# Expert weights of a mixture-of-experts layer loaded as one 8 KB piece per partition, in place of four pieces of 2 KB or two of 4 KB

## The chip, the core and the metric

The kernel runs on one core of a Trainium2 chip; the other cores are idle. The metric is the device time of one execution in microseconds (us), the median of several runs. The profile is that of one more execution.

## What is computed

One layer of a decoder over 512 tokens of width 1024, all in float32. A first half mixes tokens (an input projection, a retention branch, a recurrent branch, an output projection, a layer norm). The second half is the mixture of experts, and only it is touched here. Cut to that:

```python
expert = g_idx[:, None] * EXPERTS_PER_GROUP + top_i      # two of 32 experts for each token
...
def expert_rows(args):
    xb, e = args
    h = jax.nn.silu(xb @ w_e_gate[e]) * (xb @ w_e_up[e])   # (rows,1024) @ (1024,512), twice
    return h @ w_e_down[e]                                 # (rows,512) @ (512,1024)
...
y = jax.ops.segment_sum(y_rows * row_w[:, None].astype(y_rows.dtype), row_tok, num_segments=N + 1)[:N]
```

Each expert has three matrices of 2 MB: gate and up (1024 x 512) and down (512 x 1024). All 32 experts are read whole, 201.3 MB.

## The kernel before, in words

The kernel is written engine by engine, with semaphores set by hand. The part that matters is the expert stage.

**Loads.** SyncE (SP) issues every weight load in program order, on one DMA queue. A load (`load_m`, line 383) is 1 MB, half a matrix, and fills one of twelve buffers `m_raw` of 8 KB per partition on 128 partitions. The order is gate and up of expert 0, gate of 1, up of 1, down of 0, gate of 2, and from there for each expert e: up of e+1, down of e, gate of e+2, two loads each. The first twelve loads (ten of gate or up, two of down) are issued while the token-mixing half ends. Each later one waits until TensorE has used up the buffer it goes into (semaphore `m_done`, line 381).

**Layout.** Partition p of a load holds the rows p, p+128, p+256, ... of its half matrix, by the views `"e (k p) n -> p e k n"` of the three tensors. The row that sits on partition p has to meet the activation with the same index on the same partition, since TensorE sums over partitions.

**TensorE.** For each expert `turn_x` (line 1573) turns 64 gathered token rows `xg` into `xe` with 8 transposes, each of 128 columns of `xg`. `gate_up` (line 1590) multiplies `xe` with the four loads of gate and up. Partial sums sit in two halves of the partitions (64 rows each); ScalarE and VectorE copy them to `gu_sb`. `fold_gu` (line 1600) adds the halves and transposes in one step: 8 multiplications with a fixed matrix `fold`, where 128 columns of `gu_sb` are the operand that is loaded into the array. VectorE makes `ht` of it, and `down` (line 1612) multiplies that with the two loads of down. The order in the loop `pe_next` is gate_up(e+1), turn_x(e+2), down(e), fold_gu(e+1). A float32 multiplication is two passes in the records, so the 8 of `fold_gu` show as x16 and the 16 of `gate_up` as x32; a transpose is one.

**GpSimd.** It gathers the 64 token rows of an expert from DRAM (4 KB each) and scatters its results (2 KB each) with indirect DMAs, on a DMA queue of its own. The list of tokens for each expert is made before the stage starts.

**After the experts** the results are read back (`y_rows`, four loads of 1 MB in which a partition's 8 KB are contiguous in DRAM), weighted, added, normalised and stored.

Of the kernel before, what the change touches and what calls it, by code (L numbers as in the profile page):

```python
# [29 lines left out]
P = 128  # L30
TOKENS, D = 512, 1024
TT = TOKENS // P
KD = D // P
# [3 lines left out]
GROUPS, PER_GROUP, EXPERTS, FE = 4, 8, 32, 512  # L37
# [7 lines left out]
ROWS = 64  # L45
# [65 lines left out]
def layer(nc, io, out):  # L111
    ctx = ExitStack()
    with ctx:
# [4 lines left out]
        def at(name, kb, shape, dt=F32):  # L118

            return nc.alloc_sbuf_tensor_at(name, shape, dt, offset=BASE + int(kb * 1024))  # L120
# [48 lines left out]
        fold = at("fold", 130, [P, ROWS])  # L169
        lists_y = at("lists_y", 131, [P, LIST_COLS], I32)  # L170
        xg = at("xg", 136, [P, D])
        y_sb = at("y_sb", 140, [P, D // 2])
        gu_sb = at("gu_sb", 142, [P, 2, FE])
        silu = at("silu", 146, [P, FE // P, ROWS])
        ht = at("ht", 148, [P, FE // P, ROWS])
        bank_x = bank[:, 4, :].rearrange("p (k n) -> p k n", n=ROWS)
        bank_t = bank[:, 5, :].rearrange("p (b k n) -> p b k n", b=2, n=ROWS)
# [5 lines left out]
        def small(name, cols, dt=F32, size=4):  # L183
            t = at(name, c[0], [P, cols], dt)
            c[0] += (cols * size + 31) // 32 * 32 / 1024
            return t

        ident = small("ident", P)
# [79 lines left out]
        w_lru = io["w_lru_o"][0].rearrange("(k p) n -> p k n", p=P)  # L268
        w_ret = io["w_ret_o"][0].rearrange("(k p) n -> p k n", p=P)
        w_out = io["w_out"][0].rearrange("(k p) n -> k p n", p=P)  # L270
        w_gate = io["w_e_gate"][0].rearrange("e (k p) n -> p e k n", p=P)
        w_up = io["w_e_up"][0].rearrange("e (k p) n -> p e k n", p=P)
        w_down = io["w_e_down"][0].rearrange("e (k p) n -> p e k n", p=P)
        x_view = io["x"][0].rearrange("(t p) d -> t p d", p=P)
        out_view = out[0].rearrange("(t p) d -> t p d", p=P)

# [1072 lines left out]
        def _(pe):  # L1349
            def products(dst, pairs, first=True, last=True):  # L1350

                n = len(pairs)
                for x, (sh, sl, mh, ml) in enumerate(pairs):
                    pe.matmul(dst, sh, mh, start=first and x == 0, stop=False)  # L1354
                    pe.matmul(dst, sh, ml, start=False, stop=False)  # L1355
                    ins = pe.matmul(dst, sl, mh, start=False, stop=last and x == n - 1)  # L1356
                return ins
# [28 lines left out]
            for k in range(KD):  # L1386
                for t in range(TT):
# [4 lines left out]
                    last = pe.transpose(bank[:, k, P * t:P * t + P], x_rows[:, t, P * k:P * k + P], ident[:, :])  # L1392
# [141 lines left out]
            for t in range(TT):  # L1534
                if t >= 2:
                    pe.wait_ge(z_ok, 2 * t - 2)
                for k in range(KD):
                    if t == 0:
                        pe.wait_ge(mrg_split, k + 1)
                    for half in range(2):  # L1540
                        last = products(bank[:, 2 * (t % 2) + half, :], [
                            (mrg_hi[:, k, P * t:P * t + P], mrg_lo[:, k, P * t:P * t + P],
                             wo_hi[:, k, 512 * half:512 * half + 512], wo_lo[:, k, 512 * half:512 * half + 512])], k == 0, k == KD - 1)
# [12 lines left out]
            for t in range(TT + 1):  # L1556
                dst = bank[:, 7, 32 * t:32 * t + 32]
                for k in range(min(t + 1, TT)):
                    last = pe.matmul(dst, tri_bf[:, :] if k == t else ones_bf[:, :], mem_bf[:, 32 * k:32 * k + 32],
                                     start=k == 0, stop=k == min(t, TT - 1))  # L1560
# [5 lines left out]
            def turn_x(s, ahead=0):  # L1566

                pe.wait_ge(xg_in, 16 * s + 16 * (1 + ahead))
                if not (isinstance(s, int) and s == 0):
                    pe.wait_ge(xe_ok, s)  # L1570
                pe.sem_inc(marks, 1)
                for k in range(KD):
                    last = pe.transpose(bank_x[:, k, :], xg[0:ROWS, P * k:P * k + P], ident[0:ROWS, 0:ROWS])  # L1573
                last.then_inc(xe_turned, 1)

            def loaded_m(u):
# [17 lines left out]
            def fold_gu(s):  # L1594

                pe.wait_ge(gate_out, s + 1)
                pe.wait_ge(up_out, s + 1)
                for b in range(2):
                    for k in range(FE // P):
                        last = pe.matmul(bank_t[:, b, k, :], gu_sb[:, b, P * k:P * k + P], fold[:, :], start=True, stop=True)  # L1600
                last.then_inc(folded, 1)

            def down(s, u):
# [3 lines left out]
                for half in range(2):  # L1607
# [7 lines left out]
                    last.then_inc(m_done, 1)  # L1615

            turn_x(0)
            gate_up(0, Unit(0, ring=MRING))
            turn_x(1)
            pe.wait_ge(fold_ok, 2)  # L1620
            fold_gu(0)

            def pe_next(e, u):

                gate_up(e + 1, u)
                turn_x(e + 2)
                down(e, u.ahead(4))
                fold_gu(e + 1)
# [8 lines left out]
            with pe.If(n_over > 0):  # L1637
                with pe.Fori(0, (MAX_OVERFLOW + 1) // 2) as i:
                    for b in range(2):
                        j = 2 * i + b  # L1640
                        with pe.If(n_over > j):
                            u = Unit(M_END + 6 * b, 0, i, 12, MRING)
                            turn_x(j + (EXPERTS + 1), 1)
                            gate_up(j + EXPERTS, u, 1)
                            fold_gu(j + EXPERTS)
                            down(j + EXPERTS, u.ahead(4))
# [38 lines left out]
```

## Time and profile before

| | before |
|---|---|
| median of 3 runs | 1385.57 us (1385.32 to 1386.07) |
| profiled execution, its time | 1386.83 us |
| its span, first to last instruction | 1385.1 us |
| mean granted TensorE clock | 0.968 |
| PE busy | 1233.4 us (89%) |
| VectorE, ScalarE, GpSimd busy | 37%, 30%, 9% |
| HBM read, written | 290.02 MB, 12.65 MB |

The profiled execution is 1.3 us above the median, and 1.7 us of it lie outside the span. The token-mixing half takes the first 800 us or so, the expert stage 840 to 1345 us, and the rest is the final layer norm. Busy shares are averages over these stages. The profile has a busy row for each engine, a granted clock (1.0 is 2.4 GHz, 0.5 is 1.2 GHz), and for the DMA the number of packets, their sizes and the rate. A DMA share is the packets' own times against the time of 16 DMA engines; since one packet can begin before the last has quite ended, it can be above 100%.

### The profile page before, as it was taken

The page shows a single profiled execution, that of the slowest core. Times are in us where ns is not written, and L with a number is a line of the kernel's source. Part 1 is how long each engine was busy: PE and PEld are TensorE (multiplying, and loading weights), DVE is VectorE, ACT ScalarE, POOL GpSimd, SP SyncE. Part 2 cuts the span into 40 slices and gives each one's busy share as a digit, 9 for nine tenths or more (in the row PEclk, how much of TensorE's full clock was granted, in tenths as well). Part 3 has the DMA queues.
Part 4 walks back from the last instruction along what each step waited for, and adds up shares of the span by engine and source line. Part 5 has one row for each costly group of instructions (what it writes and reads, how often), then busy time and mean ns, then how long its engine had stood idle before and what let it go on. Part 6 is the DMA issues. An engine that isn't in the chain of part 4 may idle for free.

```text
span 1385.1 us, 16557 instructions
## 1 busy us (share of the span) xinstructions
PE 1233.4 (89%) x5880; PEld 831.3 (60%) x5880; DVE 509.1 (37%) x792; ACT 410.9 (30%) x572; POOL 126.5 (9%) x177
## 2 busy tenths in 40 slices
PE   7999999999999999999998927998888888888860
PEld 5888878878888888888887813443333333333320
DVE  5488655336373373463356430000000000000008
ACT  5767672223433333323443011111111111111111
POOL 0000000000000000000240021111111111111112
PEclk9999999999999999999999957999999999999995
DMA  7232323443232232232236356999999999999964
GB/s 234 78 109 63 90 60 88 130 137 92 62 107 78 88 91 78 73 103 79 77 120 223 142 214 221 403 401 409 407 409 406 409 403 404 404 402 400 398 233 173
DMA packets 202482, 294.25 MB, mean 212 GB/s; under 512 B 11966, under 2 KB 109486, under 8 KB 201936
## 3 DMA queue, kind: packets, MB, share of 16 engines
q1 hardware_dynamic: 196304, 283.23, 57.0%
q0 software_dynamic: 5568, 8.48, 1.7%
q10 hardware_dynamic: 576, 2.10, 0.4%
q8 instruction: 20, 0.33, 0.1%
q14 instruction: 14, 0.11, 0.0%
HBM read 290.02 MB, written 12.65 MB: 219 GB/s over the span
## 4 chain that ended last, share of the span: by engine, by line
PE 64%; DMA 18%; SPq 9%; DVE 4%; issue 2%; ACT 1%; POOL 0%; ACTq 0%; POOLq 0%; DVEq 0%
PE bank L1354 18%; PE bank L1355 17%; PE bank L1356 17%; SPq L383 9%; DMA m_raw<-in_w_e_up_dram 8%; DMA m_raw<-in_w_e_down_dram 8%; PE bank L1590 5%; PE bank L1612 4%; PE bank L1600 1%; PE bank L1528 1%; DVE x L1342 1%; DVE wo_lo L862 1%; DMA x_rows<-in_x_dram 1%; PE bank L1456 1%; DMA list_dram<-val,addr 0%
## 5 line engine op out<-in xcount | busy, mean ns | idle before, releaser
L1590 PE MATMUL bank<-m_raw,xe 128*64 128x512 f32 x1024 | 244.7, 607 | 44.2 <-DMA m_raw<-in_w_e_up_dram 37.7
L1354 PE MATMUL bank<-xt_hi,w_hi 128*128 128x512 f32 x576 | 225.1, 391 | 3.1 <-DVE w_lo L862 1.2
L1356 PE MATMUL bank<-xt_hi,w_lo 128*128 128x512 f32 x576 | 224.1, 389 | 0.0
L1355 PE MATMUL bank<-xt_lo,w_hi 128*128 128x512 f32 x576 | 224.1, 389 | 0.0
L862 DVE TENSOR_TENSOR w_lo<-raw,w_hi 128x1024 fp32r<-128x1024 f32 x120 | 148.5, 1239 | 184.6 <-ACT w_hi L578 183.3
L1590 PEld LDWEIGHTS bank<-m_raw,xe 128*64 128x64 f32 x1024 | 65.8, 137 | 197.2 <-issue 106.4
L578 ACT ACTIVATE w_hi<-raw 128x1024 fp32r<-128x1024 f32 x120 | 126.2, 1056 | 172.2 <-PE bank L1356 172.1
L1612 PE MATMUL bank<-m_raw,ht 128*64 128x512 f32 x512 | 122.4, 602 | 12.4 <-DMA m_raw<-in_w_e_down_dram 10.1
L1354 PEld LDWEIGHTS bank<-xt_hi,w_hi 128*128 128x128 f32 x576 | 108.1, 188 | 26.4 <-ACT merge L667 1.4
L1356 PEld LDWEIGHTS bank<-xt_hi,w_lo 128*128 128x128 f32 x576 | 108.1, 188 | 22.7
L1355 PEld LDWEIGHTS bank<-xt_lo,w_hi 128*128 128x128 f32 x576 | 108.2, 188 | 21.8
L1311 DVE COPY gu_sb<-bank 128x512 f32<-128x512 f32 x32 | 22.1, 692 | 265.8 <-PE bank L1590 265.8
L858 DVE TENSOR_TENSOR ht<-bank,silu 128x256 f32<-128x256 f32 x32 | 13.6, 425 | 202.9 <-ACT silu L803 183.0
L1612 PEld LDWEIGHTS bank<-m_raw,ht 128*64 128x64 f32 x512 | 33.8, 136 | 76.5 <-issue 43.1
L1600 PEld LDWEIGHTS bank<-fold,gu_sb 128*128 128x128 f32 x512 | 59.6, 191 | 25.5 <-issue 25.5
L578 ACT ACTIVATE xe<-bank 128x512 f32<-128x512 f32 x33 | 19.7, 597 | 185.4 <-PE bank L1573 185.4
L473 POOL TENSOR_TENSOR acc<-acc,g_ret 128x512 f32<-128x512 f32 x8 | 10.4, 1301 | 689.8 <-ACT g_ret L742 689.8
L1600 PE MATMUL bank<-fold,gu_sb 128*128 128x64 f32 x512 | 63.9, 278 | 0.3 <-DVE gu_sb L1311 0.3
L578 ACT ACTIVATE y_sb<-bank 128x512 f32<-128x512 f32 x32 | 19.1, 597 | 116.7 <-PE bank L1612 116.7
L578 ACT ACTIVATE gu_sb<-bank 128x512 f32<-128x512 f32 x32 | 19.1, 597 | 116.2 <-PE bank L1590 116.2
L1354 PE MATMUL bank<-w_hi,xt_hi 128*128 128x512 f32 x128 | 49.8, 389 | 0.0
L1355 PE MATMUL bank<-w_lo,xt_hi 128*128 128x512 f32 x128 | 49.8, 389 | 0.0
(229 smaller groups left out, 1632.6 us busy)
## 6 DMA issues: line engine op xcount, KB each, us to landing
m_raw<-in_w_e_gate_dram SPq DMA_DIRECT2D x64, 1024.0 KB, 15.0
m_raw<-in_w_e_up_dram SPq DMA_DIRECT2D x64, 1024.0 KB, 15.0
m_raw<-in_w_e_down_dram SPq DMA_DIRECT2D x64, 1024.0 KB, 14.1
raw<-in_w_in_dram SPq DMA_DIRECT2D x88, 512.0 KB, 4.0
raw<-in_w_ret_o_dram SPq DMA_DIRECT2D x16, 512.0 KB, 3.3
raw<-in_w_lru_o_dram SPq DMA_DIRECT2D x16, 384.0 KB, 3.0
raw<-in_w_out_dram SPq DMA_DIRECT2D x8, 512.0 KB, 3.5
y_rows<-y_dram SPq DMA_DIRECT2D x4, 1024.0 KB, 7.8
```

Source lines behind the costliest of these rows:

```text
L383: sp.dma_start(m_raw[u.slot][:, :].rearrange("p (k n) -> p k n", k=k), src).then_inc(m_loaded[u.slot], 16)
L578: return act.activation(dst, src, ACT.Copy)
L862: return dve.tensor_tensor(dst, a, b_r.bitcast(F32), ALU.subtract)
L1311: dve.tensor_copy(gu_sb[:, 1, :], bank[:, 1, :]).then_inc(up_out, 1)
L1342: step(dve.scalar_tensor_tensor(x2[:, t, :], y_rows[:, t, D * k:D * k + D], wts[:, 2 * t + k:2 * t + k + 1], x2[:, t, :], ALU.mult, ALU.add))
L1354: pe.matmul(dst, sh, mh, start=first and x == 0, stop=False)
L1355: pe.matmul(dst, sh, ml, start=False, stop=False)
L1356: ins = pe.matmul(dst, sl, mh, start=False, stop=last and x == n - 1)
L1456: last = pe.transpose(bank[:, 4 + j, P * t:P * t + P], normed[:, t, P * j:P * j + P], ident[:, :])
L1590: last = pe.matmul(bank[side:side + ROWS, b, :], xe[:, 4 * half + k, :], m_raw[v.slot][:, FE * k:FE * k + FE], start=half == 0 and k < 2, ...
L1600: last = pe.matmul(bank_t[:, b, k, :], gu_sb[:, b, P * k:P * k + P], fold[:, :], start=True, stop=True)
L1612: last = pe.matmul(bank[ROWS * b:ROWS * b + ROWS, 2, :], ht[:, 2 * half + k, :], m_raw[v.slot][:, D * k + 512 * b:D * k + 512 * b + 512], ...
```

## The change

The views of the three expert matrices now say `(p k)` in place of `(k p)`. Partition p holds the eight neighbouring rows 8p to 8p+7 of gate and up (four of down), and a load takes four (two) of them, which are 8 KB without a gap in DRAM; the next partition's piece begins 16 KB further on. So that each row still meets its activation, the two places where activations are turned onto the partitions take every eighth column of `xg` (a step of 32 bytes) and every fourth of `gu_sb` (a step of 16 bytes), where they took 128 neighbouring columns.

```diff
         xg = at("xg", 136, [P, D])
+        xg_k = xg[:, :].rearrange("r (p k) -> r k p", k=KD)
...
         gu_sb = at("gu_sb", 142, [P, 2, FE])
+        gu_k = gu_sb[:, :, :].rearrange("r b (p k) -> r b k p", k=FE // P)
...
-        w_gate = io["w_e_gate"][0].rearrange("e (k p) n -> p e k n", p=P)
-        w_up = io["w_e_up"][0].rearrange("e (k p) n -> p e k n", p=P)
-        w_down = io["w_e_down"][0].rearrange("e (k p) n -> p e k n", p=P)
+        w_gate = io["w_e_gate"][0].rearrange("e (p k) n -> p e k n", p=P)
+        w_up = io["w_e_up"][0].rearrange("e (p k) n -> p e k n", p=P)
+        w_down = io["w_e_down"][0].rearrange("e (p k) n -> p e k n", p=P)
...
-                    last = pe.transpose(bank_x[:, k, :], xg[0:ROWS, P * k:P * k + P], ident[0:ROWS, 0:ROWS])
+                    last = pe.transpose(bank_x[:, k, :], xg_k[0:ROWS, k, :], ident[0:ROWS, 0:ROWS])
...
-                        last = pe.matmul(bank_t[:, b, k, :], gu_sb[:, b, P * k:P * k + P], fold[:, :], start=True, stop=True)
+                        last = pe.matmul(bank_t[:, b, k, :], gu_k[:, b, k, :], fold[:, :], start=True, stop=True)
```

On SP, among the first twelve loads, these rows stand before the change. A row is a line of the kernel, the instruction, its destination and source, and the shape that it moves (partitions, then the counts of the steps within one); the number behind `m_raw` tells its buffers apart, and `x_dram<-x_95` are the stores of the tokens between them.

```order
L383 DMA m_raw_101<-in_w_e_gate_dram 128x4x512
L383 DMA m_raw_102<-in_w_e_gate_dram 128x4x512
L405 DMA x_dram<-x_95 128x1024 x2
L383 DMA m_raw_103<-in_w_e_up_dram 128x4x512
L383 DMA m_raw_104<-in_w_e_up_dram 128x4x512
L405 DMA x_dram<-x_95 128x1024
L383 DMA m_raw_105<-in_w_e_down_dram 128x2x1024
L383 DMA m_raw_106<-in_w_e_down_dram 128x2x1024
```

At the same place on SP, with the change:

```order
L385 DMA m_raw_101<-in_w_e_gate_dram 128x2048
L385 DMA m_raw_102<-in_w_e_gate_dram 128x2048
L407 DMA x_dram<-x_95 128x1024 x2
L385 DMA m_raw_103<-in_w_e_up_dram 128x2048
L385 DMA m_raw_104<-in_w_e_up_dram 128x2048
L407 DMA x_dram<-x_95 128x1024
L385 DMA m_raw_105<-in_w_e_down_dram 128x2048
L385 DMA m_raw_106<-in_w_e_down_dram 128x2048
```

No row has moved. The shape of a load went from four runs of 512 numbers (or two of 1024) on a partition to one of 2048.

On TensorE, at the end of the expert stage (last turn, down of expert 30, fold and down of expert 31), before the change:

```order
L1573 MATMUL bank<-ident,xg 128x64 x8
L1612 MATMUL bank<-m_raw_105,ht 64x512 x4
L1612 MATMUL bank<-m_raw_106,ht 64x512 x4
L1600 MATMUL bank<-fold,gu_sb 128x64 x8
L1612 MATMUL bank<-m_raw_107,ht 64x512 x4
L1612 MATMUL bank<-m_raw_108,ht 64x512 x4
```

The same place with the change:

```order
L1575 MATMUL bank<-ident,xg 128x64 x8
L1614 MATMUL bank<-m_raw_105,ht 64x512 x4
L1614 MATMUL bank<-m_raw_106,ht 64x512 x4
L1602 MATMUL bank<-fold,gu_sb 128x64 x8
L1614 MATMUL bank<-m_raw_107,ht 64x512 x4
L1614 MATMUL bank<-m_raw_108,ht 64x512 x4
```

Nothing moved here either, and counts and shapes are the same; the rows do not show the new steps within `xg` and `gu_sb`. The line numbers are two higher for the two new lines of code.

## Rows read from the trace of the kernel before

**Rows 1.** The page, part 2: 40 equal slices of the span (34.6 us each)

```profile
PEclk9999999999999999999999957999999999999995
DMA  7232323443232232232236356999999999999964
GB/s 234 78 109 63 90 60 88 130 137 92 62 107 78 88 91 78 73 103 79 77 120 223 142 214 221 403 401 409 407 409 406 409 403 404 404 402 400 398 233 173
```

**Rows 2.** The page, part 4: the chain that ended last, by line

```profile
PE bank L1354 18%; PE bank L1355 17%; PE bank L1356 17%; SPq L383 9%; DMA m_raw<-in_w_e_up_dram 8%; DMA m_raw<-in_w_e_down_dram 8%; PE bank L1590 5%; PE bank L1612 4%; PE bank L1600 1%; PE bank L1528 1%; DVE x L1342 1%; DVE wo_lo L862 1%; DMA x_rows<-in_x_dram 1%; PE bank L1456 1%; DMA list_dram<-val,addr 0%
```

**Rows 3.** Timeline of PE near 905 us: start, length, instructions

```profile
903.24 2.00 PE L1600 MATMUL bank<-fold,gu_sb 128*128 128x64 f32 x16
905.17 7.09 PE L1590 MATMUL bank<-m_raw,xe 128*64 128x512 f32 x32
912.18 0.71 PE L1573 MATMUL bank<-ident,xg 64*128 64x64 f32 x8
912.82 3.65 PE L1612 MATMUL bank<-m_raw,ht 128*64 128x512 f32 x16
916.40 2.00 PE L1600 MATMUL bank<-fold,gu_sb 128*128 128x64 f32 x16
```

**Rows 4.** Timeline of PE near 1210 us, idle time and its releaser in brackets

```profile
1204.55 2.00 PE L1600 MATMUL bank<-fold,gu_sb 128*128 128x64 f32 x16
...
1211.75 1.94 PE L1590 MATMUL bank<-m_raw,xe 128*64 128x512 f32 x8 [0.79 <-DMA m_raw<-in_w_e_up_dram]
...
1221.10 2.00 PE L1600 MATMUL bank<-fold,gu_sb 128*128 128x64 f32 x16
```

**Rows 5.** DMA queues, 843 to 1334 us: packets, MB, share of 16 engines

```profile
DMA packets 83984, 196.44 MB, mean 400 GB/s; under 512 B 5815, under 2 KB 5815, under 8 KB 83980
...
q1 hardware_dynamic: 79092, 188.48, 99.2%
q0 software_dynamic: 4888, 7.91, 4.4%
```

**Rows 6.** DMA queues, 947 to 949 us

```profile
DMA packets 408, 0.82 MB, mean 409 GB/s; under 512 B 9, under 2 KB 9, under 8 KB 408
...
q1 hardware_dynamic: 408, 0.82, 105.0%
```

**Rows 7.** DMA queues, 969 to 970 us

```profile
DMA packets 111, 0.42 MB, mean 420 GB/s; under 512 B 6, under 2 KB 6, under 8 KB 111
```

**Rows 8.** DMA queues, 1351 to 1359 us, while `y_rows` is read

```profile
DMA packets 465, 3.42 MB, mean 427 GB/s; under 512 B 48, under 2 KB 48, under 8 KB 48
...
q1 hardware_dynamic: 465, 3.42, 101.0%
```

**Rows 9.** DMA queues, 1336 to 1339 us

```profile
q1 hardware_dynamic: 22, 0.08, 6.7%
```

**Rows 10.** Weight loads of `fold_gu` and `turn_x`: ns min/median/max

```profile
L1600 PEld LDWEIGHTS bank<-fold,gu_sb x512: 186/192/192, 850.6 to 1338.0; 128*128 128x128 f32 x171
...
L1573 PEld LDWEIGHTS bank<-ident,xg x264: 134/138/222, 838.4 to 1331.8; 64*128 64x128 f32 x132
```

**Rows 11.** The chain in order of time, start and end of the expert stage

```profile
838.48 1.10 PE bank L1573 x8
...
850.59 1.97 PE bank L1600 x16
...
1336.38 1.94 PE bank L1600 x16
...
1338.76 0.44 DVE ht L858
...
1339.24 3.68 PE bank L1612 x16
```

## The prediction

> **What bounds the kernel now.** I read the page's forty slices first, to see which stage can answer to the change at all. Only the expert stage reads these matrices. In thirteen slices in a row the DMA runs at 398 to 409 GB/s with nine or more tenths busy, at full TensorE clock [rows 1]; everywhere earlier it is far below that. The chain names `m_raw` transfers (8% and 8%) and SP's issuing of them (9%) ahead of the matmuls that use them [rows 2].
>
> Then TensorE, since it is 89% busy over the whole span and could be the real bound. Near 905 us it runs without a gap: from one `fold_gu` to the next 13.16 us [rows 3]. That is its own pace for an expert, while it lives on the twelve loads fetched ahead. Near 1210 us the same distance is 16.55 us, with waits for loads in between [rows 4]. Over the stage, 31 steps from the fold at 850.59 to that at 1336.38 take 485.8 us [rows 11], 15.67 us each. So TensorE has 2.5 us of slack in each expert, and the transfers set the pace.
>
> Then the DMA itself. From 843 to 1334 us SP's queue moved 188.48 MB [rows 5]. Loads of 1.0486 MB make that 180, which are all but the first twelve: 118 of gate or up, 62 of down. Its packets fill 99.2% of 16 engines' time and GpSimd's another 4.4%, 103.6% together; a full stretch shows 105.0% [rows 5, 6]. On the mean little is idle. And the last stretch shows why the mean matters less than one engine: from 1336 to 1339 us there are 6.7% busy, one engine in sixteen (6.25%), still working alone [rows 9]. A load counts as landed when its slowest engine is done, and that engine has no gap to give. Its time is packets times time of a packet.
>
> So the price of a packet by its size decides. I looked for stretches of one size:
> - 2 KB: 408 packets in 2 us, of which 9 are small. 399 in 2 us on 16 engines is 80.2 ns each, 409 GB/s [rows 6].
> - 4 KB: 105 packets in 1 us, nearly all of this size, 420 GB/s [rows 7]. 4096 B at 420/16 GB/s is 156.0 ns.
> - 8 KB: the kernel has this form already. `y_rows` gives 465 less 48 packets in 8 us, 307.0 ns each, 427 GB/s [rows 8].
>
> The three agree with a fixed part of some 4.5 ns and 75.6 ns for each 2 KB. The first is what the change removes.
>
> **The change, part by part.**
> Pieces: the shape of a load becomes 128x2048, which is how `y_rows` is read and how its 8 KB packets arise. A gate or up load was 512 packets, 32 on each engine, 32 x 80.2 = 2.566 us. It becomes 8 x 307.0 = 2.456 us: 0.110 us less, 118 times, 13.0 us. A down load was 16 x 156.0 = 2.496 us, and becomes 2.456: 0.040 us less, 62 times, 2.5 us. Sum 15.5 us. The first twelve loads gain too but lie before 843 us, under the making of the lists, and count for nothing.
>
> A page sets the ceiling lower. The Trainium skill, DMA: Bandwidth & Descriptors, section "iDMA fabric — 4 AXI ports for 8 engines, asymmetric across TPBs", gives 408.7 GB/s for one load stream from SP with 1 MiB per DMA and 4 KiB rows; were that the ceiling of any such stream, pieces over 2 KB would gain nothing and the time would stay near 1385.6. The trace disagrees: it has 420 with 4 KB and 427 with 8 KB pieces.
>
> Other traffic: the gathers and scatters keep their packets (7.91 MB [rows 5]). They now stand behind packets of 307 in place of 80 ns where queues alternate. GpSimd issues a gather almost one expert ahead of its use, and I cost this at nothing; it would matter only if a gather's wait grew by several us. SP has a quarter as many pieces to issue; that earns nothing, since its queue is already full.
>
> The new operand steps: each expert has 16 weight loads of `gu_sb` columns and 8 of `xg` columns whose neighbours now lie 16 and 32 bytes apart. No row of this kernel shows such a load. Now, fold passes come every 121 ns (1.93 us for 16) and transposes every 80 ns (0.64 us for 8) [rows 3]. Below, the step is free: 0. Above, I take a weight load's whole record, 192 and 138 ns [rows 10], as doubled and not overlapped: 16 x 0.192 + 8 x 0.138 = 4.2 us for each expert. I take 60 ns for each load, half of a fold's slot, 1.4 us for an expert: nearer to nothing, since loads run ahead of matmuls. In the middle of the stage that lies inside the slack of 2.5 us, which the quicker transfers shrink to about 2.0. At the two ends it is on the path. `turn_x(0)` stands before the first buffer comes free (8 x 0.06 = 0.5 us). The fold of expert 31 stands between the late loads and `ht` at 1339.20, and the last matmuls start at once behind that [rows 11]: 16 x 0.06 = 1.0 us. Since the last load arrives at about the same time, nothing else covers it.
>
> Sum: 15.5 - 1.5 = 14.0 us off the profiled execution's 1386.83, so 1372.8. That execution is 1.3 us above the median, so 1371.6 as a median; I say 1371.5.
>
> **The rivals.**
> *Half the gain.* Reading 8 KB at every 16 KB from HBM may not run as the gapless `y_rows` does. Were it only as good as 4 KB packets now, gate and up give 0.070 x 118 = 8.3 us, down nothing, less 1.5: 1378.8. For it: no row shows this pitch. Against: the source today also jumps between pieces, and both sizes keep their rate.
>
> *No gain.* The stream could be capped near 409 GB/s by something that only long streams meet, `y_rows` being 4 MB. Then 1385.6 plus at most 1.5. Against: the 420 GB/s stretch stands inside the long stream [rows 7]. That the pieces are not joined at all would end here too, but the shape says they are.
>
> *Slower: TensorE becomes the bound through the stepped weight loads.* The pace of 13.16 us grows by 24 loads times their extra. At 83 ns each it meets the transfers' new pace (15.67 - 0.50); from 104 ns on, when 2.5 us are used up, the kernel is slower than before. With the upper bound, 4.2 us, an expert takes 17.35 us, 1.68 more than now, 31 times: 52 us, 1438. For it: TensorE has the least slack of all engines, and a fold's slot (121 ns) is already above a transpose's (80 ns) although both load 128 columns. Against: what is needed is more than a doubling of the transpose's slot. The Trainium skill, Advanced Engine Details and Errata, section "SBUF Cachelines", speaks for this rival: it says that reads which reach a different 16-byte line each time pay a penalty, and both new steps do; it names no size. No run here shows it.
>
> **How the numbers follow.** I give the forecast 0.66, half the gain 0.12, no gain 0.10, slower 0.12. The forecast's own range is 1367 to 1377. Its upper end is the sum with the weight loads at the point where TensorE begins to limit (83 ns, 0.5 us more) and another third of the gain lost in mixed traffic. Its lower end lies between free steps (1370.1) and packets without any fixed part (303 ns in place of 307: 5 us further, 1365). The range reaches to 1381 to take in the half gain. Two runs of this kernel differ by under 0.1%, and 0.2% (2.8 us) is what a measurement can tell from no change. Faster by more than that: forecast and half gain, 0.78; within: 0.10; slower: 0.12.
>
> **What would show it.** Right, if: SP's queue shows some 26,000 packets in the stage (180 x 128 of 8 KB and the small ones that end a load), where it has 79,092 [rows 5]; a full stretch of the loads runs at 425 GB/s or more; the distance between folds near 1210 us is about 0.5 us shorter; the stage from the first to the last fold is 14 to 16 us shorter. The steps cost what I took if 16 fold passes need about 2.9 us and 8 transposes 1.1 us. Wrong, if: packets of 8 KB take well over 310 ns in the middle of the stage; the packets stay at 2 KB; or PE runs without gaps at 1210 us, which is the slower rival.

## The result, and the profile after

The change makes the kernel slower: 1435.33 us (1432.87 to 1437.33) against 1385.55, medians of four runs each, a ratio of 1.0359 with a 95% interval of 1.0342 to 1.0376. The span of the profiled execution is 1435.5 us, and its mean granted clock 0.928 where it was 0.968.

The slices of the page, as in [rows 1], now 35.9 us each:

```profile
PEclk9999999999999999999999669999999889999985
DMA  7233122533232232232344639999999999999904
GB/s 225 76 105 98 51 77 88 162 92 100 74 103 84 63 102 73 88 88 74 98 168 204 234 136 379 376 382 392 380 384 387 381 391 379 381 380 383 377 15 173
```

The expert stage moves 376 to 392 GB/s where it moved 398 to 409. By this row alone one would blame the new loads. The chain of work that ended last, as in [rows 2], says otherwise:

```profile
PE bank L1592 19%; PE bank L1356 17%; PE bank L1358 17%; PE bank L1357 17%; PE bank L1602 9%; PE bank L1614 8%; PE bank L1575 2%; PE bank L1530 1%; DVE x L1344 1%; DVE wo_lo L864 1%; DMA x_rows<-in_x_dram 1%; PE bank L1458 0%; DMA list_dram<-val,addr 0%; DVE x L1171 0%; POOL list_dram L495 0%
```

No `m_raw` transfer is left in it. Gate_up (now L1592), fold (L1602), down (L1614) and turn (L1575) fill it instead. The timeline of PE near 1210 us, which answers to [rows 3] and [rows 4]:

```profile
1211.24 3.99 PE L1602 MATMUL bank<-fold,gu_sb 128*128 128x64 f32 x16
1215.16 8.61 PE L1592 MATMUL bank<-m_raw,xe 128*64 128x512 f32 x32
1223.70 1.09 PE L1575 MATMUL bank<-ident,xg 64*128 64x64 f32 x8
1224.72 3.65 PE L1614 MATMUL bank<-m_raw,ht 128*64 128x512 f32 x16
1228.30 3.99 PE L1602 MATMUL bank<-fold,gu_sb 128*128 128x64 f32 x16
```

TensorE runs without a gap, and from fold to fold it takes 17.06 us; alone it took 13.16 [rows 3]. By the starts of the rows the fold takes 3.92 us (1.93 before), the turn 1.02 (0.64), gate_up 8.54 (7.01), down 3.58 as before. So 1.99 + 0.38 + 1.53 = 3.9 us were added. The first two are the stepped weight loads; their records, as in [rows 10]:

```profile
L1602 PEld LDWEIGHTS bank<-fold,gu_sb x512: 307/329/330, 851.4 to 1385.4; 128*128 128x128 f32 x171
...
L1575 PEld LDWEIGHTS bank<-ident,xg x264: 182/202/207, 838.7 to 1378.0; 64*128 64x128 f32 x132
```

The third was foreseen nowhere, for gate_up reads nothing with a step. The windows of one microsecond, with busy times of PE, PEld, DVE, ACT and POOL, then the granted clock, the DMA share and GB/s, show it:

```profile
1214.00:1215.00 1.00, 1.00 (x6) 1.00 (x5) 0.00 (x0) 0.00 (x0) 0.29 (x1) 0.92 0.98 262
1215.00:1216.00 1.00, 1.00 (x3) 0.34 (x5) 0.32 (x1) 0.38 (x1) 0.00 (x0) 0.50 0.97 356
1216.00:1217.00 1.00, 1.00 (x6) 0.31 (x4) 0.11 (x1) 0.00 (x0) 0.00 (x0) 0.50 1.05 442
1217.00:1218.00 1.00, 1.00 (x6) 0.38 (x4) 0.00 (x0) 0.00 (x0) 0.00 (x0) 0.50 0.98 410
1218.00:1219.00 1.00, 1.00 (x6) 0.28 (x6) 0.00 (x0) 0.00 (x0) 0.00 (x0) 0.87 1.00 418
```

Near the end of the fold the clock goes from 1.0 (2.4 GHz) to 0.5 (1.2 GHz) and stays there a little over 3 us, in which gate_up runs at half speed. Before, the clock was at 1.00 in every stretch read from 860 to 1300 us, also where TensorE had no gap either, so a TensorE without gaps is not by itself what brings it down. One such stretch of the kernel before, then one of the changed kernel:

```profile
900.00:910.00 10.00, 10.00 (x56) 4.42 (x54) 0.42 (x1) 1.94 (x4) 2.32 (x4) 1.00 1.04 397
...
1200.00:1250.00 50.00, 50.00 (x216) 24.75 (x214) 3.10 (x6) 6.53 (x12) 7.06 (x12) 0.91 0.99 380
```

The pieces did become what the order of loads said. The DMA queues from 848 to 1357 us, as in [rows 5]:

```profile
DMA packets 30256, 193.66 MB, mean 380 GB/s; under 512 B 5661, under 2 KB 5661, under 8 KB 7564
...
q1 hardware_dynamic: 25534, 185.89, 94.2%
```

25,534 packets on SP's queue, and 94.2% where 99.2% was full. And what SP waited for from 860 to 1350 us (us in total, times, longest):

```profile
SPq L385 <- PE bank L1592: 289.1, 115, 7.0
SPq L385 <- PE bank L1614: 103.8, 58, 2.5
```

SP stands waiting for TensorE to free buffers. The bound has changed sides.

### The profile page after: what moved, and what is told of

It is laid out like the page before. It is cut to its first block, busy times and chain, and to the rows that moved or that the text cites. A ratio compares the mean times of both kernels' runs of the same rounds, so it can differ in the third digit from the quotient of the medians.

```text
span 1435.5 us, 16557 instructions
## 1 busy us (share of the span) xinstructions
PE 1339.2 (93%) x5880; PEld 923.5 (64%) x5880; DVE 508.9 (35%) x792; ACT 411.0 (29%) x572; POOL 126.3 (9%) x177
## 4 chain that ended last, share of the span: by engine, by line
PE 91%; DVE 4%; DMA 2%; issue 1%; ACT 1%; POOL 0%; ACTq 0%; POOLq 0%; SPq 0%; DVEq 0%
PE bank L1592 19%; PE bank L1356 17%; PE bank L1358 17%; PE bank L1357 17%; PE bank L1602 9%; PE bank L1614 8%; PE bank L1575 2%; PE bank L1530 1%; DVE x L1344 1%; DVE wo_lo L864 1%; DMA x_rows<-in_x_dram 1%; PE bank L1458 0%; DMA list_dram<-val,addr 0%; DVE x L1171 0%; POOL list_dram L495 0%
## 5 line engine op out<-in xcount | busy, mean ns | idle before, releaser
L1592 PE MATMUL bank<-m_raw,xe 128*64 128x512 f32 x1024 | 278.3, 705 | 0.7 <-ACT xe L580 0.7
L1592 PEld LDWEIGHTS bank<-m_raw,xe 128*64 128x64 f32 x1024 | 82.3, 163 | 172.1 <-issue 167.9
L1602 PEld LDWEIGHTS bank<-fold,gu_sb 128*128 128x128 f32 x512 | 121.9, 328 | 25.2 <-issue 25.2
L1602 PE MATMUL bank<-fold,gu_sb 128*128 128x64 f32 x512 | 127.6, 403 | 0.0
L1614 PE MATMUL bank<-m_raw,ht 128*64 128x512 f32 x512 | 119.6, 610 | 0.9 <-DVE ht L860 0.9
L1614 PEld LDWEIGHTS bank<-m_raw,ht 128*64 128x64 f32 x512 | 34.6, 139 | 60.0 <-issue 56.8
L1575 PEld LDWEIGHTS bank<-ident,xg 64*128 64x128 f32 x264 | 31.6, 199 | 46.4 <-issue 46.4
L1575 PE MATMUL bank<-ident,xg 64*128 64x64 f32 x264 | 36.1, 278 | 20.2 <-DMA xg<-x_dram,x_idx 20.2
L1356 PE MATMUL bank<-w_hi,xt_hi 128*128 128x512 f32 x128 | 49.8, 389 | 0.0
```

Of the source, the lines that this page charges most:

```text
L1575: last = pe.transpose(bank_x[:, k, :], xg_k[0:ROWS, k, :], ident[0:ROWS, 0:ROWS])
L1592: last = pe.matmul(bank[side:side + ROWS, b, :], xe[:, 4 * half + k, :], m_raw[v.slot][:, FE * k:FE * k + FE], start=half == 0 and k < 2, ...
L1602: last = pe.matmul(bank_t[:, b, k, :], gu_k[:, b, k, :], fold[:, :], start=True, stop=True)
L1614: last = pe.matmul(bank[ROWS * b:ROWS * b + ROWS, 2, :], ht[:, 2 * half + k, :], m_raw[v.slot][:, D * k + 512 * b:D * k + 512 * b + 512], ...
```

## The experiments

Each ran on the chip with the kernel before beside it, which had medians of 1386.22, 1386.89 and 1387.16 us in the three groups of runs (four experiments each). A ratio is to that one, with its 95% interval.

### The two halves of the change, apart

**pieces_only**, against the changed kernel:

```diff
-                    last = pe.transpose(bank_x[:, k, :], xg_k[0:ROWS, k, :], ident[0:ROWS, 0:ROWS])
+                    last = pe.transpose(bank_x[:, k, :], xg[0:ROWS, P * k:P * k + P], ident[0:ROWS, 0:ROWS])
...
-                        last = pe.matmul(bank_t[:, b, k, :], gu_k[:, b, k, :], fold[:, :], start=True, stop=True)
+                        last = pe.matmul(bank_t[:, b, k, :], gu_sb[:, b, P * k:P * k + P], fold[:, :], start=True, stop=True)
```

> The 8 KB pieces alone: the loads are those of the change, but the turns and the folds read neighbouring columns as before, so rows and activations are paired wrongly and the output is not the layer's. Theory (the pieces are worth what the prediction summed, and the stepped weight loads on TensorE took it back): 15.5 us faster than before, 1370; distance between folds 15.0 to 15.2 us late in the stage, no clock below 1.0 there. Rival (8 KB pieces at a pitch of 16 KB are themselves slow; the changed kernel moves only 380 GB/s): 1400 or more.

Measured: 1374.62 us, ratio 0.9924 (0.9907 to 0.9940). Two stretches of it (columns as above), then a row of its PE timeline:

```profile
950.00:1000.00 50.00, 44.73 (x234) 17.35 (x232) 4.04 (x7) 7.12 (x13) 7.24 (x13) 1.00 1.01 418
...
1250.00:1300.00 50.00, 43.34 (x222) 16.50 (x218) 3.35 (x6) 6.53 (x12) 7.07 (x12) 1.00 1.01 414
```

```profile
1208.81 1.94 PE L1614 MATMUL bank<-m_raw,ht 128*64 128x512 f32 x8 [0.40 <-DMA m_raw<-in_w_e_down_dram]
```

The clock is 1.0, TensorE waits for loads again, and the loads run at 414 to 418 GB/s. The pieces make the kernel faster. By the ratio they are worth 10.5 us (8.3 to 12.9), not 15.5; that third is taken up below.

**steps_only**, against the changed kernel:

```diff
-        w_gate = io["w_e_gate"][0].rearrange("e (p k) n -> p e k n", p=P)
-        w_up = io["w_e_up"][0].rearrange("e (p k) n -> p e k n", p=P)
-        w_down = io["w_e_down"][0].rearrange("e (p k) n -> p e k n", p=P)
+        w_gate = io["w_e_gate"][0].rearrange("e (k p) n -> p e k n", p=P)
+        w_up = io["w_e_up"][0].rearrange("e (k p) n -> p e k n", p=P)
+        w_down = io["w_e_down"][0].rearrange("e (k p) n -> p e k n", p=P)
```

> The stepped reads alone: turns and folds read every eighth and every fourth column as in the change, the loads are those of before, so the pairing is wrong and the output is not the layer's. Theory: TensorE is the bound at 17.06 us for an expert whatever the pieces, so 1435 as with the change, fold passes 245 ns apart, clock at 0.5 for a part of gate_up. Rival (the slow loads of the change come from the pieces): near 1386.

Measured: 1435.02 us, 1.0348 (1.0324 to 1.0372): the whole loss, with the loads of before. Its PE timeline near 1215 us:

```profile
1211.17 4.00 PE L1602 MATMUL bank<-fold,gu_sb 128*128 128x64 f32 x16
...
1228.24 4.00 PE L1602 MATMUL bank<-fold,gu_sb 128*128 128x64 f32 x16
```

The same 17.07 us for an expert. The stepped reads alone set the time, whatever the pieces. A stretch of it:

```profile
1200.00:1250.00 50.00, 50.00 (x216) 24.69 (x214) 3.17 (x6) 6.53 (x12) 7.04 (x12) 0.91 1.03 388
```

The DMA share is 1.03, nearly the 1.04 of before, though only 388 GB/s are moved and TensorE is the bound. So a full DMA share does not show that the transfers set the pace; the gaps of TensorE that end with a load [rows 4] do.

### Which step: the turn's or the fold's

**gate_up_only**, against the changed kernel:

```diff
-        w_down = io["w_e_down"][0].rearrange("e (p k) n -> p e k n", p=P)
+        w_down = io["w_e_down"][0].rearrange("e (k p) n -> p e k n", p=P)
...
-                        last = pe.matmul(bank_t[:, b, k, :], gu_k[:, b, k, :], fold[:, :], start=True, stop=True)
+                        last = pe.matmul(bank_t[:, b, k, :], gu_sb[:, b, P * k:P * k + P], fold[:, :], start=True, stop=True)
```

> Gate and up in 8 KB pieces with the stepped turn, down and the fold as before; the output is the layer's. Theory: TensorE's own pace is 13.16 + 0.38 = 13.5 us, below the transfers' 15.2, so the 13.0 us of the gate and up pieces stay, less 0.4 for the first turn: 1373. Rival (any stepped weight load brings the clock down, as in the change): TensorE's pace 15.1 us or more with a clock below 1.0, 1384 or slower.

Measured: 1378.41 us, 0.9947 (0.9931 to 0.9964), faster than before. It is some 5 us short of the 1373 expected, about what pieces_only lacks too. A stretch, and the turn:

```profile
1150.00:1200.00 50.00, 44.52 (x225) 17.96 (x225) 3.78 (x7) 6.91 (x13) 8.09 (x13) 1.00 1.02 412
```

```profile
1208.24 1.09 PE L1575 MATMUL bank<-ident,xg 64*128 64x64 f32 x8
```

The stepped turn costs its 0.38 us in the slack, and brings no clock down.

**down_only** keeps the other half: `w_gate` and `w_up` and the turn are set back as in the two diffs above, `w_down` and the fold stay changed.

> Down in 8 KB pieces with the stepped fold, gate, up and the turn as before; the output is the layer's. Two theories of the lost 1.5 us in gate_up: if the slow folds (3.9 us of few columns streamed) bring the clock down, TensorE's pace is 13.16 + 1.99 + 1.52 = 16.7 us for an expert, 31 x 1.0 us over 15.67, so about 1417. If the clock fell for another reason (turn and fold together), the pace is 15.15 us, hidden below the transfers: 1383 to 1387.

Measured: 1415.18 us, 1.0208 (1.0191 to 1.0226), close to the 1417 of the first theory. Two experts in a row on PE:

```profile
1200.83 8.78 PE L1592 MATMUL bank<-m_raw,xe 128*64 128x512 f32 x32
...
1213.77 3.95 PE L1602 MATMUL bank<-fold,gu_sb 128*128 128x64 f32 x16
1217.65 7.09 PE L1592 MATMUL bank<-m_raw,xe 128*64 128x512 f32 x32
```

One gate_up takes 8.78 us, the next 7.09: the fold is equally slow each time, but the clock does not fall behind every one. From gate_up to gate_up an expert with the quick gate_up takes 15.17 us, less than the 15.67 of before (6 of 30), and the others 16.5 to 16.8. So the stepped fold without the fall of the clock would have stayed within the slack, and its own 2 us are not what makes this kernel slower.

### Is the clock a term of its own

**split_fold**, against the changed kernel (`fold_gu` takes a part; the first needs only the gate copy):

```diff
                 turn_x(e + 2)
+                pe.wait_ge(ht_ok, e + 1)
+                fold_gu(e + 1, 0)
                 down(e, u.ahead(4))
-                fold_gu(e + 1)
+                fold_gu(e + 1, 1)
```

> The changed kernel, but in the loop the fold's eight passes for gate are issued ahead of down and those for up behind it, each still stepped; the output is the layer's. Theory (it is the unbroken 3.9 us of slow folds that brings the clock down): two stretches of 2 us with 3.6 us of down between them keep the clock at 1.0, gate_up stays at 7.0 us, TensorE's pace is 13.16 + 1.99 + 0.38 = 15.5 us: 1380 to 1384. Rival (the clock follows the mean activity of an expert's whole period, or the slow loads wherever they stand): gate_up 8.5 us, 1435 as with the change.

Measured: 1418.78 us, 1.0223 (1.0208 to 1.0239), between the two. Neither holds as stated: some experts are as quick as the theory said, and the others lose the time of a slow clock, but in another place than the rival said. Two stretches with the granted clock (third number from the end):

```profile
1150.00:1200.00 50.00, 50.00 (x207) 23.92 (x206) 2.66 (x5) 6.03 (x12) 6.86 (x11) 0.90 1.00 377
1200.00:1250.00 50.00, 50.00 (x234) 27.18 (x232) 4.04 (x7) 7.12 (x13) 7.83 (x14) 1.00 1.01 411
```

From the PE timeline, one expert of each stretch:

```profile
1158.70 7.09 PE L1592 MATMUL bank<-m_raw,xe 128*64 128x512 f32 x32
1165.71 1.09 PE L1575 MATMUL bank<-ident,xg 64*128 64x64 f32 x8
1166.74 2.13 PE L1603 MATMUL bank<-fold,gu_sb 128*128 128x64 f32 x8
1168.80 5.22 PE L1616 MATMUL bank<-m_raw,ht 128*64 128x512 f32 x16
1173.95 2.08 PE L1603 MATMUL bank<-fold,gu_sb 128*128 128x64 f32 x8
1175.96 2.37 PE L1592 MATMUL bank<-m_raw,xe 128*64 128x512 f32 x10
...
1208.77 7.09 PE L1592 MATMUL bank<-m_raw,xe 128*64 128x512 f32 x32
...
1218.83 3.65 PE L1616 MATMUL bank<-m_raw,ht 128*64 128x512 f32 x16
...
1224.42 7.09 PE L1592 MATMUL bank<-m_raw,xe 128*64 128x512 f32 x32
```

Gate_up to gate_up is 17.26 us in the first and 15.65 us in the second, with the same instructions. The difference is in down, behind turn and half a fold (5.22 in place of 3.65). Its windows there show the clock:

```profile
1167.00:1168.00 1.00, 1.00 (x6) 1.00 (x6) 0.00 (x0) 0.44 (x1) 0.18 (x1) 1.00 1.01 401
1168.00:1169.00 1.00, 1.00 (x6) 0.88 (x7) 0.00 (x0) 0.00 (x0) 0.89 (x1) 0.79 1.01 426
1169.00:1170.00 1.00, 1.00 (x4) 0.33 (x4) 0.00 (x0) 0.00 (x0) 0.08 (x1) 0.50 0.97 410
```

The clock falls here behind the turn and half a fold, 3.1 us of stepped loads, so an unbroken 3.9 us is not needed for it. 15.65 us is an expert's time with the stepped loads and no fall of the clock, the same as in the kernel before (15.67), and a fall adds 1.5 to 1.7 us where it comes. Parting the slow folds spares it to 12 of 30 experts. Which experts are spared, with the same instructions in each, stays open.

### How wide the step may be

**fold_step2** and **fold_step8** leave the kernel before as it is but for the fold's operand:

```diff
-                        last = pe.matmul(bank_t[:, b, k, :], gu_sb[:, b, P * k:P * k + P], fold[:, :], start=True, stop=True)
+                        last = pe.matmul(bank_t[:, b, k, :], gu_2[:, (b + k) % 4, 0:P], fold[:, :], start=True, stop=True)
```

where `gu_2` has neighbours 8 bytes apart (`gu_8` 32 bytes, likewise).

> The kernel before, with only the fold reading every second column (8 bytes apart, two to a line of 16 bytes); the columns are the wrong ones, so the output is not the layer's. Theory after the Trainium skill's rule on 16-byte lines in Advanced Engine Details and Errata: two reads to a line are free, passes 121 ns apart, 1386. Rival (any step on the loaded operand costs): passes 180 to 245 ns, and at 245 the time of a stepped fold, 1417.

> The kernel before, with only the fold reading every eighth column (32 bytes apart); the columns are the wrong ones, so the output is not the layer's. Theory (each read of a new line costs the same, however far): passes 245 ns apart as at 16 bytes, clock falls, pace 16.7 us, 1417. Rival (the cost grows with the step): over 245 ns, 1430 or more. Second rival (at 32 bytes it is only what the turn showed, 48 ns more): 170 ns and 1386.

Measured: 1386.94 us for the step of 8 bytes, 0.9995 (0.9985 to 1.0004), and 1420.74 us for 32 bytes, 1.0240 (1.0225 to 1.0256). A fold of each:

```profile
1220.29 2.10 PE L1601 MATMUL bank<-fold,gu_sb 128*128 128x64 f32 x16
```

```profile
1216.72 4.02 PE L1601 MATMUL bank<-fold,gu_sb 128*128 128x64 f32 x16
```

By the starts of the rows behind them a pass costs 127 ns at 8 bytes and 246 ns at 32, against 121 at 4 and 245 at 16. It is a jump between 8 and 16 bytes, not a slope; nothing between the two was tried. The time at 32 bytes is near the 1417 expected, and 35 us over what the rival with 170 ns said. The Trainium skill, Advanced Engine Details and Errata, section "SBUF Cachelines", says that at least two hits on a 16-byte line are needed for full performance. The runs agree but for the 6 ns that a pass costs more at 8 bytes, and show the size of the penalty for this load.

### Keeping the pieces without the slow fold

**evict_order**, against the changed kernel: the copies out of the banks put `gu_sb` into the pieces' order, so that the fold is contiguous.

```diff
-                copy(gu_sb[:, 0, :], bank[:, 0, :]).then_inc(gate_out, 1)
+                copy(gu_sb[:, 0, :].rearrange("r (k p) -> r k p", p=P), bank[:, 0, :].rearrange("r (p k) -> r k p", p=P)).then_inc(gate_out, 1)
...
-                dve.tensor_copy(gu_sb[:, 1, :], bank[:, 1, :]).then_inc(up_out, 1)
+                dve.tensor_copy(gu_sb[:, 1, :].rearrange("r (k p) -> r k p", p=P), bank[:, 1, :].rearrange("r (p k) -> r k p", p=P)).then_inc(up_out, 1)
...
-                        last = pe.matmul(bank_t[:, b, k, :], gu_k[:, b, k, :], fold[:, :], start=True, stop=True)
+                        last = pe.matmul(bank_t[:, b, k, :], gu_sb[:, b, P * k:P * k + P], fold[:, :], start=True, stop=True)
```

> All three matrices in 8 KB pieces and the layer's output, but ScalarE and VectorE put gu_sb into the order of the pieces when they copy it (they read the bank with a step of 16 bytes), so that the fold loads neighbouring columns as before; the turn keeps its step. Theory (only the stepped fold hurts): TensorE's own pace 13.5 us, fold passes 121 ns apart, no clock below 1.0, and the time of the pieces alone (1374.6) plus up to 1.5 us for the first turn and slower copies: 1374 to 1377. Rival: the stepped copies take over 1.4 us each and come onto the path: 1385 or more.

Measured: 1377.18 us, 0.9928 (0.9914 to 0.9942). The records of the copies and a fold:

```profile
L580 ACT ACTIVATE gu_sb<-bank x32: 597/597/597, 848.5 to 1317.0; 128x512 f32<-128x512 f32 x32
L1313 DVE COPY gu_sb<-bank x32: 691/692/693, 851.9 to 1322.0; 128x512 f32<-128x512 f32 x32
```

```profile
1214.46 2.00 PE L1602 MATMUL bank<-fold,gu_sb 128*128 128x64 f32 x16
```

ScalarE and VectorE read the bank with a step of 16 bytes in the very time of before (medians of 597 and 691 ns there too). The time is at the upper end of what was expected, and the rival, copies of 1.4 us, is out.

**whole_halves** makes each load one contiguous megabyte, and so the steps smaller:

```diff
-        w_gate = io["w_e_gate"][0].rearrange("e (k p) n -> p e k n", p=P)
+        w_gate = io["w_e_gate"][0].rearrange("e (h p k) n -> p e h k n", h=2, p=P)
...
-                    last = pe.transpose(bank_x[:, k, :], xg[0:ROWS, P * k:P * k + P], ident[0:ROWS, 0:ROWS])
+                    last = pe.transpose(bank_x[:, k, :], xg_h[0:ROWS, k // 4, k % 4, :], ident[0:ROWS, 0:ROWS])
...
-                        last = pe.matmul(bank_t[:, b, k, :], gu_sb[:, b, P * k:P * k + P], fold[:, :], start=True, stop=True)
+                        last = pe.matmul(bank_t[:, b, k, :], gu_h[:, b, k // 2, k % 2, :], fold[:, :], start=True, stop=True)
```

(this one against the kernel before; `w_up` and `w_down` alike, `expert` takes the half's number, `xg_h` steps 16 bytes, `gu_h` 8).

> Another layout with 8 KB pieces and the layer's output: each half matrix is one contiguous megabyte, partition p holds its rows 4p to 4p+3 (2p and 2p+1 of down), so the next partition's piece follows without a gap. The turn then takes every fourth column (16 bytes), the fold every second (8 bytes). Theory (pitch of the pieces doesn't matter, a fold at 8 bytes takes 2.03 us as in the run with that step): as with the copies in the pieces' order, 1375 to 1378, clock 1.0. Rival (the 5 us of the sum that the pieces alone didn't give are lost to the 16 KB pitch): 1370 to 1373, and 427 GB/s in full stretches inside the stage where the pieces alone show less.

> The same kernel as the run with the copies in the pieces' order, once more, to stand beside whole_halves on the same chip: 1377, or 0.993 of before.

Measured on one chip: 1376.05 us, 0.9922 (0.9909 to 0.9935), and 1377.05 us, 0.9928 (0.9911 to 0.9945). A stretch of 200 us of whole_halves:

```profile
1000.00:1200.00 200.00, 182.43 (x916) 76.08 (x914) 14.28 (x26) 27.67 (x51) 30.20 (x52) 1.00 1.01 417
```

417 GB/s, as the other has there. The intervals overlap: the pitch of 16 KB costs nothing that can be told (at most some 4 us by the intervals), and both kernels beat the one before and the changed one. The turn of this kernel, with a step of 16 bytes:

```profile
1208.72 1.17 PE L1575 MATMUL bank<-ident,xg 64*128 64x64 f32 x8
```

By the start of the row behind it, 1209.81, a transpose takes 136 ns at 16 bytes, where it takes 128 at 32 and 80 without a step.

### Where a third of the pieces' gain goes

**before_few_rows** and **pieces_few_rows** take the indirect row traffic away, once from the kernel before and once from pieces_only:

```diff
-            last_x, last_y = pool.to_reg(TOKENS - 1), pool.to_reg(4 * TOKENS - 1)
+            last_x, last_y = pool.to_reg(0), pool.to_reg(0)
```

> The kernel before with its gathers and scatters cut to token row 0 (all other rows are skipped, and the final read takes 4 MB of expert weights in place of the results), so nearly no row moves beside the weight loads; the output is not the layer's. 180 loads at 2.566 or 2.496 us are 457.6 us, against 496 us now from 843 us to the last landing: about 1348. It is the base for pieces_few_rows.

> The 8 KB pieces alone (neighbouring columns, wrong pairing) with the same cut of gathers and scatters; the output is not the layer's. Theory (the third of the gain that is missing is lost where rows and 8 KB pieces mix): the gain over before_few_rows is the full 15.5 us, near 1333. Rival (8 KB packets of a long stream are themselves slower than those of y_rows): the gain stays near 10.5 us, 1338, and packets over 309 ns appear with no rows beside them.

Measured: 1356.25 us, 0.9786 (0.9769 to 0.9803), and 1342.07 us, 0.9668 (0.9654 to 0.9682). The pieces are now worth 16.4 us by the ratios (about 13 to 19), where pieces_only gained 10.5, and 14.2 by the medians, where it gained 11.6. In the profiled executions the stretch from the first pass of the first fold to the last pass of the last is 16.4 us shorter with the pieces (440.9 against 457.3), and with the rows 11.6 us (475.8 against 487.4). So the sum's 15.5 us are there without the rows; how much of them the rows take is known only roughly. The DMA queues from 1000 to 1200 us, of before_few_rows:

```profile
DMA packets 36859, 82.23 MB, mean 411 GB/s; under 512 B 3371, under 2 KB 3371, under 8 KB 36859
```

of pieces_few_rows:

```profile
DMA packets 13854, 85.19 MB, mean 426 GB/s; under 512 B 3457, under 2 KB 3457, under 8 KB 3457
...
q1 hardware_dynamic: 11694, 85.18, 100.8%
```

of pieces_only, with its rows (q0 is GpSimd's queue):

```profile
DMA packets 12980, 83.23 MB, mean 416 GB/s; under 512 B 2417, under 2 KB 2417, under 8 KB 3221
...
q0 software_dynamic: 2000, 3.28, 4.7%
```

and of the kernel before, in the same 200 us:

```profile
DMA packets 34729, 81.28 MB, mean 406 GB/s; under 512 B 2347, under 2 KB 2347, under 8 KB 34729
```

Without rows the stream of 8 KB pieces keeps 426 GB/s for 200 us, the rate of `y_rows`: 13,854 packets less the 3,457 small ones on 16 engines are 307.8 ns each, against 307.0 there. The rival, that packets of a long stream are slower, is out. With rows the total is 416 GB/s, the rows' own bytes counted in, and the kernel before has 411 without and 406 with them. So with rows the total of the 8 KB stream is 10 GB/s lower (2.3%) and that of the old one 5 (1.2%). The difference, 1.1% of a stage of some 490 us, is 5.4 us by this estimate, the size of the missing third. What in the mixing of rows and pieces costs it was not found. Both kernels were expected 8 to 9 us faster than they are; the base was reckoned from the clean packet prices, and what else they wait for was not looked into.

## Why the prediction was wrong

Wrong in sign: 1371.5 forecast with 0.78 for faster, 1435.3 measured, outside the range. Its steps in turn:

- *What bounds the kernel now*: right. Transfers set the pace, TensorE had 2.5 us of slack for an expert, and in pieces_only and the two runs with few rows the time moved with the packets. Of its evidence the gaps that end with a load carry this; a full DMA share does not, for steps_only has it too.
- *The sum of the pieces*, "13.0" and "2.5" us: right as prices of packets (pieces_few_rows: 14 to 16 us), too large by about a third in the kernel as it is (10.5). The term that failed is "I cost this at nothing" for the packets of gathers and scatters between the 8 KB ones. (The lower bound of the range has a slip too: 303 in place of 307 ns for 8 packets of 180 loads are 5.8 us, not 5. Nothing hangs on it.)
- *"I take 60 ns for each load, half of a fold's slot"*: the step that failed first. The fold's cost 124 ns each, the turn's 48, together 2.37 us for an expert in place of 1.44. It was about right for the turn and half of what the fold costs. It was taken "nearer to nothing, since loads run ahead of matmuls"; but the fold's passes came 121 ns apart before and 245 ns with the step, so its loads were not hidden behind them.
- *The clock, which the sum did not have at all*: the step that decided. 2.37 us alone are within the slack of 2.5: the experts of split_fold whose clock did not fall take 15.65 us, the same as before, and those of down_only 15.17. What made the kernel slower is the 1.53 us for each expert that gate_up lost at 1.2 GHz, some 47 us over 31 of them; 49.8 were lost in all. The prediction priced instructions one by one and never asked what 3.9 us of slow weight loads do to the granted clock of what follows. Why the clock falls behind them stays open.
- *The rival "TensorE becomes the bound through the stepped weight loads"*: right in place and in the sign that it named (PE without gaps at 1210 us), given 0.12, and right in mechanism for the loads; it did not have the clock. Its 1438 lies close to 1435 partly by luck: it had 4.2 us from doubled load records, where the runs showed 2.4 us of loads and 1.5 us of clock. Its threshold of 104 ns for each load also bears out: the mean over the 24 was 99 ns, and without the fall of the clock that came out even with before.
- *Half the gain* by the pitch, and *no gain* by a ceiling near 409: refuted by the 426 GB/s of pieces_few_rows, which has the pitch and a long stream; whole_halves, without the pitch, is no quicker beyond its interval. The 408.7 GB/s of the Trainium skill, DMA: Bandwidth & Descriptors, section "iDMA fabric — 4 AXI ports for 8 engines, asymmetric across TPBs", is no ceiling here, as the 420 with 4 KB pieces [rows 7] already showed.

## What to carry to other kernels

A layout that makes a transfer better often makes an engine read with a step; count the slack of that engine first, and try the stepped operand by itself, with the old transfers, before judging the transfers. For float32 operands that are loaded into TensorE's array, keep neighbours at most 8 bytes apart, or put them in order in a copy that is made anyway. And where TensorE's slack is short, a slower stretch costs more than its own length if the clock falls behind it: read the granted clock of the stage, not only the lengths of the instructions.

## What the runs showed of the hardware that was not expected

- A pass of the fold, with a weight load of 128 float32 columns on 128 partitions, takes 121, 127, 245 and 246 ns at 4, 8, 16 and 32 bytes between neighbours. The transposes, one pass each with a load on 64 partitions, go from 80 to 136 ns at 16 bytes and 128 at 32. Why they suffer less was not tried.
- Behind 3.9 us of such loads, with PE busy in every record, the granted clock fell from 2.4 to 1.2 GHz for a little over 3 us. With folds of 1.9 us the stretches read here stand at 1.00, without gaps on PE too (900 to 910 us). With the fold in two halves, the fall came behind 3.1 us of stepped loads, for some experts and not for others; with the turn alone stepped (1.0 us) it did not come.
- The same copy from the bank with a step of 16 bytes costs ScalarE and VectorE nothing (597 and 692 ns).
- The packet times in clean stretches of 2, 4 and 8 KB (80.2, 156.0 and 307.0 ns, in the prediction) fit a fixed part of about 4.5 ns. Gathers and scatters of 3.3 MB in 200 us bring the expert loads beside them from 85.18 to 79.95 MB with 8 KB packets (6.1%), and from 82.22 to 78.15 MB with those of before (5.0%); what in their mixing does it stays open.
- The DMA share stayed at 1.02 to 1.03 in steps_only while 375 to 388 GB/s were moved and TensorE set the pace, where before it was 1.04 at 402 to 403.
